# Layer 0's parameters moved, one more unsplit gate, and attention with two products per head and quarter turns

## The reference

```python
xn = rmsnorm(x, norm1_g)
cq, ckv, k_rope, u, gate_a, gate_b = split(xn @ w_in)        # 256, 128, 32, 512, 1024, 1024 columns
# branch A: 8 heads; q from cq, k (64 columns) and v (64) from ckv, 32 rotary columns shared in k
q, k = rmsnorm per head, rotary part turned
attn = softmax(q @ k.T / sqrt(96)) @ v ;  A = attn @ w_attn_up
# branch B: diagonal complex state space, 32 groups of 16 channels, 64 states, both directions
y = Re(C_f s_f) + Re(C_b s_b) + D * u ;  z = gelu(y) @ w_glu ;  B = z[:, :1024] * sigmoid(z[:, 1024:])
x = x + (sigmoid(gate_a) * A + sigmoid(gate_b) * B) @ w_o
x = x + (silu(h @ w_ffn_gate) * (h @ w_ffn_up)) @ w_ffn_down      # h = rmsnorm(x, norm2_g)
```

## Time and profile before

| | |
|---|---|
| median of 3 runs (range) | 1619.85 us (1618.29 to 1621.41) |
| the profiled execution | 1616.31 us, its span 1614.5 us |
| mean granted TensorE clock | 0.986 |
| busy: TensorE, VectorE, ScalarE, GpSimd | 1550.9, 884.8, 591.3, 557.8 us |
| instructions | 21071 |
| moved by DMA | 188.34 MB, mean 117 GB/s |

### The profile page before, as it was taken

The page is one execution under the profiler, slowest core; times in us unless marked ns, Lnnn a source line. Parts: engine busy times, 40 slices in busy tenths (PEclk is TensorE's granted clock), DMA queues, the critical chain, the costliest instruction groups (busy, mean ns, idle before and its releaser), DMA issues.

```text
span 1614.5 us, 21071 instructions
## 1 busy us (share of the span) xinstructions
PE 1550.9 (96%) x8352; PEld 1230.3 (76%) x8352; DVE 884.8 (55%) x1233; ACT 591.3 (37%) x992; POOL 557.8 (35%) x274
## 2 busy tenths in 40 slices
PE   8996998999999989999999899888999999999999
PEld 3554787778878877888888788777887888888887
DVE  5998477758547997558231862576684222112210
ACT  4561227653344231333331323676424223122220
POOL 0000013235434454434442333422434444434442
PEclk9998899999999999999999999999999999999999
DMA  7457720032232244453526362101422332322232
GB/s 253 157 173 258 277 88 1 1 105 91 92 120 91 79 148 155 147 160 91 169 96 246 117 231 89 50 1 40 118 79 91 105 104 82 101 91 95 88 104 79
DMA packets 73201, 188.34 MB, mean 117 GB/s; under 512 B 23568, under 2 KB 32144, under 8 KB 69008
## 3 DMA queue, kind: packets, MB, share of 16 engines
q1 hardware_dynamic: 43968, 145.18, 26.6%
q10 hardware_dynamic: 29136, 41.82, 8.0%
HBM read 154.47 MB, written 32.51 MB: 116 GB/s over the span
## 4 chain that ended last, share of the span: by engine, by line
PE 71%; DVE 15%; DVEq 5%; ACT 3%; DMA 2%; issue 2%; SPq 1%; POOL 0%; ACTq 0%; POOLq 0%
PE ps L1623 22%; PE ps L1624 22%; PE ps L1625 22%; PE ps L1767 2%; DVE qkTl L1479 1%; DVE nmx L1511 1%; DVE work L1036 1%; SPq L414 1%; ACT prob L945 1%; PE ps L1930 1%; DMA ctd_scr<-CPp 1%; PE ps L1921 1%; DVEq L1205 1%; DVEq L1163 1%; DVE work L1037 1%
## 5 line engine op out<-in xcount | busy, mean ns | idle before, releaser
L500 POOL TENSOR_TENSOR wl<-stage,wh 128x1024 fp32r<-128x1024 f32 x204 | 511.2, 2510 | 917.8 <-ACT wh L562 910.6
L562 ACT ACTIVATE wh<-stage 128x1024 fp32r<-128x1024 f32 x211 | 221.6, 1056 | 350.3 <-PE ps L1625 240.8
L1623 PE MATMUL ps<-xg2h,wh 128*128 128x512 f32 x704 | 280.7, 399 | 2.6 <-DVE act L1595 2.6
L1625 PE MATMUL ps<-xg2h,wl 128*128 128x512 f32 x704 | 279.1, 396 | 0.0
L1624 PE MATMUL ps<-xg2l,wh 128*128 128x512 f32 x704 | 279.0, 396 | 0.0
L1623 PEld LDWEIGHTS ps<-xg2h,wh 128*128 128x128 f32 x704 | 132.6, 188 | 35.5 <-issue 3.9
L1625 PEld LDWEIGHTS ps<-xg2h,wl 128*128 128x128 f32 x704 | 132.7, 188 | 32.2
L1624 PEld LDWEIGHTS ps<-xg2l,wh 128*128 128x128 f32 x704 | 132.8, 189 | 32.0 <-issue 0.5
L1623 PE MATMUL ps<-hidh,wh 128*128 128x512 f32 x352 | 139.8, 397 | 2.3 <-DVE hidl L1601 1.2
L1625 PE MATMUL ps<-hidh,wl 128*128 128x512 f32 x352 | 139.2, 396 | 0.0
L1624 PE MATMUL ps<-hidl,wh 128*128 128x512 f32 x352 | 139.2, 396 | 0.0
(11 more groups left out here) (271 smaller groups left out, 2840.4 us busy)
## 6 DMA issues: line engine op xcount, KB each, us to landing
stage<-in_stream SPq DMA_DIRECT2D x211, 512.0 KB, 3.2
CPTR<-ctd_scr ACTq DMA_DIRECT2D x6, 1664.0 KB, 10.3
slabs<-in_stream SPq DMA_DIRECT2D x16, 512.0 KB, 6.0
InT<-in_scr ACTq DMA_DIRECT2D x6, 1024.0 KB, 6.3
ctd_scr<-CPp SPq DMA_DIRECT2D x4, 1152.0 KB, 8.2
ctd_scr<-CPp ACTq DMA_DIRECT2D x4, 1152.0 KB, 6.6
in_scr<-BPI SPq DMA_DIRECT2D x4, 1024.0 KB, 5.1
in_scr<-BPI ACTq DMA_DIRECT2D x4, 1024.0 KB, 3.9
```

The lines of the kernel that those rows point to most:

```text
L500: pool.tensor_tensor(wl[:, s, :], stage[:, (n - RAW) % STAGES, :], wh[:, s, :].bitcast(F32), ALU.subtract).then_inc(wl_ready, 1)
L562: return act.activation(o, i, ACT.Copy, **kw)
L1623: pe.matmul(o, wt[0], x[0], start=start, stop=False)
L1625: return pe.matmul(o, wt[1], x[0], start=False, stop=stop)
```

## The change

Two groups of edits.

*Layer 0's front.* `RAW` becomes S_GATE + 10: slab 17 is an unsplit gate too. `BB`, `Call` and `pwi` move into the place of `xgl`, so VectorE's `normed_x` waits for the last taps (`k_ps`). `CPp`, `rot`, `pwc` lie in `CPTR[1]`'s place, `Kf` in `Toep[1]`'s; `InT[1]` and `U[1]` are free from the start, and SyncE loads them right after block 2's maps are stored. The taps of blocks 2 and 3 are stored from ScalarE's queue. Two slabs are loaded ahead of the waits in SyncE's queue. Inputs, outputs and states are set one gate later in the orders of TensorE and VectorE.

*Attention.* `vh` and `vl` become one tensor `vv` with four slots of 64 columns: high of head 0, low of head 0, low of head 1, high of head 1. A head's two slots together are one stationary operand of 128 columns; `pTh` and `pTl` pass through it once each. A bank then holds the high part's product in one half of the partitions and the low part's in the other. ScalarE copies the low half across (`other`), VectorE adds it (`added`), GpSimd scales (`scaled`) and makes `oTl` (`output`), but for the last pair, where VectorE does both. GpSimd also norms the keys of pairs 1 to 3. The probability-value product stands in odd units from 5 on. The turns come a quarter per unit, at units 3 to 6 on TensorE and ScalarE, 4 to 7 on VectorE. At the end the up projection's products of the first two slabs with pairs 0 to 2 are taken before the last pair's are ready, three of them before the last probability-value product.

```diff
-RAW = S_GATE + 9
+RAW = S_GATE + 10
...
-            ra = Region(ffn_top if l else set_at[1])
-            if l == 0:
-                CPp.append(ra.take(f"CPp{l}", [P, CPN]))
+            ra = Region(ffn_top if l else KT * SEQ * 4)
             BB.append(ra.take(f"BB{l}", [P, 2, C32, 2 * GCH]))
             Call.append(ra.take(f"Call{l}", [P, BLOCKS, 2, C8 * GCH]))
-            Kf.append(ra.take(f"Kf{l}", [P, 2, KW]))
+            pwi.append(ra.take(f"pwi{l}", [P, 2, C32, CHUNK]))
+            if l == 0:
+                assert ra.at <= XGB
+                ra = Region(set_at[1] + 4 * (INT + CTD))
+                Kf.append(ra.take(f"Kf{l}", [P, 2, KW]))
+                ra = Region(set_at[1] + 4 * INT)
+                CPp.append(ra.take(f"CPp{l}", [P, CPN]))
...
@@ SyncE
             store_cp(2)
+            load_input(1)
             store_turns()
-            store_input_map(3)
-            store_taps(2)
             load_output(0)
             load_taps(0)
+            store_input_map(3)
             store_cp(3)
-            for i in range(2):
-                sp.wait_ge(in_stored[i], 32)
+            staged_slab(RAW + 2)
+            staged_slab(RAW + 3)
             sp.wait_ge(k_ps, BLOCKS)
             sp.wait_ge(cp_stored, 16 * BLOCKS)
-            load_input(1)
             load_output(1)
-            store_taps(3)
             sp.wait_ge(k_stored, 128 * BLOCKS)
             load_taps(1)
...
@@ GpSimd
+                def normed_keys(hp):
+                    inv = ast[:, hp, 1, :].rearrange("p (t h) -> p t h", h=2)
+                    pool.wait_ge(qkT_ps, 4 * (PAIRS * l + hp))
+                    pool.tensor_tensor(KW_[:, :, :, 0:NOPE], ...)
+                    pool.tensor_tensor(KW_[:, :, :, NOPE:QK], ...)
+                    pool.drain().then_inc(k_normed, 1)
+
+                def scaled(hp):
+                    n = PAIRS * l + hp
+                    pool.wait_ge(r_copied, n + 1)
+                    pool.wait_ge(o_added, 2 * n + 2)
+                    pool.tensor_tensor(of[:], of[:], Rn[:], ALU.mult)
+                    pool.drain().then_inc(o_scaled, 1)
+
+                def output(hp):
+                    pool.wait_ge(oh_ready, PAIRS * l + hp + 1)
+                    pool.tensor_tensor(oTl[:, hp, :], of[:], oTh[:, hp, :].bitcast(F32), ALU.subtract).then_inc(o_ready, 1)
...
                         if u == 2:
                             rotated()
+                            normed_keys(hp + 1)
...
+                    if hp and a < STEPS:
+                        if u == 6:
+                            scaled(hp - 1)
+                    if a >= 2 * UNITS and u == 0:
+                        output(hp - 2)
...
@@ ScalarE
-                    split(0, S_GATE + 9)
+                    gain_slab(17)
+                    split(0, S_GATE + 10)
                     gate_out(6)
-                    split(0, S_GATE + 10)
+                    store_taps(0, 2)
+                    split(0, S_GATE + 11)
                     taps(0, 3)
                     gate_out(7)
-                    split(0, S_GATE + 11)
+                    store_taps(0, 3)
...
+                def other(hp, h):
+                    n = PAIRS * l + hp
+                    act.wait_ge(pv_done, 4 * n + 2 * h + 2)
...
+                    copy(oth[h * VD:(h + 1) * VD, :], ps[(1 - h) * VD:(2 - h) * VD, 4 + h, :]).then_inc(o_other, 1)
...
-                        if u in (4, 6):
-                            turned(hp + 1, u - 4)
+                        if 3 <= u < 7:
                             turned(hp + 1, u - 3)
...
+                    if a >= UNITS and u == 1:
+                        other(hp - 1, 0)
                     if a >= UNITS and u == 2:
                         scales(hp - 1)
                     if a >= UNITS and u == 4:
-                        output(hp - 1)
+                        other(hp - 1, 1)
+                    if a >= 2 * UNITS and u == 0:
+                        output(hp - 2)
...
@@ VectorE, layer 0
-                    remainder(S_GATE + 9)
                     remainder(S_GATE + 10)
+                    dve.wait_ge(k_ps, BLOCKS)
                     for k in range(KT):
                         normed_x(0, k)
                     direct_taps(0, 3)
                     dve.wait_ge(in_stored[0], 32)
                     gate(8)
+                    remainder(S_GATE + 11)
+                    gate(9)
                     states(0)
-                    gate(9)
-                    remainder(S_GATE + 11)
+                    gate(10)
                     remainder(S_GATE + 12)
                     states(1)
...
@@ VectorE, attention
+                def added(hp, h):
+                    n = PAIRS * l + hp
+                    half = slice(h * VD, (h + 1) * VD)
+                    if hp:
+                        dve.wait_ge(o_ready, n)
+                    dve.wait_ge(o_other, 2 * n + h + 1)
+                    tt(of[half, :], ps[half, 4 + h, :], oth[half, :], ADD).then_inc(o_added, 1)
...
+                    if a >= UNITS and u == 2:
+                        added(hp - 1, 0)
+                    if a < STEPS and hp and u == 5:
+                        added(hp - 1, 1)
+                    if a < STEPS and hp + 1 < PAIRS and u >= 4:
+                        turned(hp + 1, u - 4)
...
@@ TensorE, layer 0
                     inputs(0)
+                    gate(9)
                     for k in range(KT):
                         pe.wait_ge(xl_ready, k + 1)
-                    gate(9)
+                    gate(10)
                     inputs(1)
-                    gate(10)
+                    gate(11)
                     outputs(0)
-                    gate(11)
+                    gate(12)
                     outputs(1)
-                    gate(12)
                     inputs(2)
...
@@ TensorE, attention
-                        if hp + 1 < PAIRS and u in (4, 6):
-                            if u == 4 and hp:
+                        if hp + 1 < PAIRS and 3 <= u < 7:
+                            if u == 3 and hp:
                                 pe.wait_ge(r_copied, n)
-                            turn(hp + 1, (u - 4) // 2)
+                            turn(hp + 1, u - 3)
...
-                    if a >= 4 and a % 2 == 0:
-                        m = (a - 4) // 2
+                    if a == STEPS + 2:
+                        ready(S_UP)
...
+                        for k in range(PAIRS - 1):
+                            up_product(0, 0, k)
+                    if a >= 5 and a % 2:
+                        m = (a - 5) // 2
...
                         for t in range(TT):
-                            last = products(ps[:, 4 + h, tok], (vh[pair % 2][:, t, :], vl[pair % 2][:, t, :]),
-                                            (pTh[:, m % 2, t, :], pTl[:, m % 2, t, :]), t == 0, t == TT - 1)
+                            v = vv[pair % 2][:, t, 2 * h:2 * h + 2, :].rearrange("p a d -> p (a d)")
+                            pe.matmul(ps[:, 4 + h, tok], v, pTh[:, m % 2, t, :], start=(t == 0), stop=False)
+                            last = pe.matmul(ps[:, 4 + h, tok], v, pTl[:, m % 2, t, :], start=False, stop=(t == TT - 1))
                         last.then_inc(pv_done, 1)
```

More of the change, by code:

```diff
@@ L63 @@
 UP_ORDER = [(c, k) for c in range(2) for k in range(PAIRS)]
-UP_FIRST = [(c, k) for c in range(2) for k in range(PAIRS - 1)] + [(c, PAIRS - 1) for c in range(2)]
 QKV = 2 * (QK + NOPE + VD)
@@ L231, in build @@
         Rn = spare.take("Rn", [P, SEQ])
+        oth = spare.take("oth", [P, SEQ])
         of = RS
@@ L452, in _ @@
             sp.dma_start(Call[0][:].rearrange("p b r c -> p (b r c)"), cmat[0]).then_inc(call_loaded, 16)
-            for n in range(3, RAW - 1):
+            for n in range(3, RAW - 2):
                 raw(n)
             store_cp(0)
-            raw(RAW - 1)
+            raw(RAW - 2)
             staged_slab(RAW)
             staged_slab(RAW + 1)
+            raw(RAW - 1)
             store_input_map(0)
@@ L1894, in _, with up_product @@
                 pe.wait_ge(qk_sq, 8 * (l + 1))
-                turn(0, 0)
-                turn(0, 1)
+                for i in range(4):
+                    turn(0, i)
                 pe.wait_ge(qk_sqa, 8 * (l + 1))
-                for a in range(STEPS + 3):
+                def up_product(j, c, k):
+                    if j == 0:
+                        pe.wait_ge(o_ready, PAIRS * l + k + 1)
+                    return products(ps[:, 2 * j + c, :], weight(l, S_UP + j, k * 2 * P + c * P, P),
+                                    (oTh[:, k, :], oTl[:, k, :]), k == 0, k == PAIRS - 1)
+                for a in range(STEPS + 4):
                     hp, u = a // UNITS, a % UNITS
```

114 lines of the change are left out of this document (61 added, 53 removed).

## The result

The changed kernel took **1594.4 us** in the median of 4 runs (1593.2 to 1599.5), the kernel before 1619.1; ratio 0.986 (0.983 to 0.988). On two other chips, beside later experiments, it had 1602.1 (6 runs, ratio 0.990) and 1598.7 us (5 runs, 0.988). The profiled execution took 1599.5 us (span 1597.7 against 1614.5).

What follows compares the result with a forecast made beforehand. TensorE, busy 96% of the span, bounds the kernel, losing time mainly in layer 0's front and attention. 1616.3 - 22 (front) - 27 (attention) = 1567.3, plus 3.5 to the median: 1571 us, range 1560 to 1590.

Steps and rivals of the forecast that it cites:

- cost nothing unless the loads slip too: Layer 0's front: taps stores of blocks 2 and 3 from ScalarE's queue, some 5 us each, delay nothing TensorE needs soon.
- the slow clock's 10 us: Layer 0, 134 to 199 us: with the waits gone the low granted clock goes too, gaining 10 us.
- Rival 2: DMA still holds layer 0: block 1's states or maps late, about 10 us return, 1581 us; chance 0.12.
- The three waits of the earlier trace: Layer 0: TensorE's waits for `xgl` (5.48 us), `U` and `InT` (5.98) and `S` (3.45) vanish, 14.9 us.
- the sum of 22 us: Layer 0's front: net gain 23.5 us less 1.5 for new small waits; bounds 12 and 24.
- Rival 3: TensorE back to back, full gain in both parts (bounds 24 and 2 x 16): 1560 us; chance 0.08.
- Two products instead of three: Attention: eight probability-value matmuls a step for 12, 0.50 us less in 16 steps, 8.0 us of TensorE work per layer.
- the 5.5 forecast for the waits: Attention: lost time per layer goes from 17.7 to about 12.2 us; with 8.0 of work, 13.5 us per layer.
- The other 12.7 shrink to about 7: Attention: of 17.7 us lost per layer about 5 are pipeline filling and stay; the remaining waits shrink to about 7.
- lies under nine W_up products, a cost of zero there: Attention's tail: its longer chain, some 3.3 us, is covered by 6.3 us of products; 3 us if cover failed.
- rival 4: Attention: VectorE and GpSimd block each other at a shared port, period 8 us longer, 64 in all, 1635 us; chance 0.02.
- the narrow form: VectorE and GpSimd: port sharing hurts only VectorE instructions with two SBUF inputs, so the forecast of 1571 us stands.

Runs made afterwards that it cites:

- latents: Changed kernel with, in layer 0, the last block's Toep products ahead of the latents' third turn and VectorE's first turned latents made earlier; 1593.5 us.
- fronts: Changed kernel with block 2's taps stored from SyncE's queue, and Toep products and first turned latents moved earlier in both layers; 1585.4 us (0.979).
- all: Changed kernel with both layers' front edits, the gated-product edits and attention's reordered turns with VectorE's maximum left first; 1568.8 us (0.970).
- the taps kernel: Changed kernel with block 2's taps stores issued from SyncE's queue, ahead of block 0's output maps, instead of from ScalarE's; 1591.0 us (0.983).
- the third pass: Changed kernel with the first probability-value matmul issued twice, so 12 matmuls a step again; 1603.9 us (0.990).
- the order changed: Changed kernel with turn banks swapped, VectorE's turned remainder behind the maximum but ahead of additions, first addition and one GpSimd `oTl` later; 1593.9 us (0.985).
- the gated product kernel: Changed kernel with two `yT` loads ahead of the last `oTh`, `gyh` made by ScalarE, fourth Gelu ahead of a slab's split; 1598.7 us.

## Why the prediction was wrong, by its steps

**The taps stores "cost nothing unless the loads slip too": failed.** I looked for who stands behind the issuing, in ScalarE's queue, and priced that at nothing. The cost is at the landing: one `Kf`, so copy, addition and eviction of a gate wait for it. 7.7 us with the slow clock behind it (248.7 to 241.0 with the stores from SyncE), a net figure of two profiled executions: the wait of 1.93 us for `InT` goes too, and the pause for `latTl` grows by 2.0.

**Gain of the slow clock's 10 us, "a clock of 1.00 from 134 to 200": not met in the changed kernel (0.89 from 134 to 153, behind the wait for the gate's bank), met once the stores were moved, and then the loss stood further on.** With the three waits gone, TensorE reached the third turn of the latents before VectorE had made room; VectorE's last states step is stretched beside GpSimd's remainders (the scans and the first product behind them take 4.46 and 2.65 us at 203.3 and 207.9, in the block before 2.34 and 0.69). That this stretch makes the pause is argued, not tried; what was tried is the order of `latTl` and of the taps products, with which the pause is 0.1 us (latents), 0.7 (fronts) and 1.25 (all). The pause is 1.5 to 3.7 us, and in some executions the clock falls behind it: 7.0 us between the taps kernel and fronts (241.0 to 234.0). With 1.0 us left over, that is all of the front's 15.7. Rival 2 named DMA as the holder, at 10 us, through block 1's states or maps; half of the loss did hang on a DMA's landing, but on that of a store out of a single buffer, and the other half on VectorE's order.

**The front's other steps: right.** The three waits of the earlier trace rows are gone, `InT` is asked for early, and the sum of 22 us is met (234.0 against 233) by the kernel without those two. Rival 3's 1560 us was mis-added: bounds of 24 and 2 x 16 off the median of 1619.9 give 1564.

**Two products instead of three, 8.0 us of TensorE work a layer: right in work, but half of it was covered.** 64 matmuls are gone in each layer (529 to 461 in the stretch, with other groups' edges), a step of eight takes 1.03 us; putting them back costs 3.9. So this term, 8.0 in the sum, was worth 3.9 in the kernel as it ran: with the third pass back, the waits for `qkTl` (0.76 and 0.83 us) are gone, so without it they took part of the place of the work. That kernel with the third pass is still 5.8 and 5.5 us shorter than before to the first gated product, as the 5.5 forecast for the waits.

**"The other 12.7 shrink to about 7": too small by some 3.5 us.** This is the same shortfall seen from the other side. Named waits for `Rn` and `QW` came as priced (1.15 and 1.67 against 0.8 and 1.8). Missing were the waits at the second use of a turn bank, behind VectorE's addition in unit 5 (0.76 and 0.83 us, one in each of the third and fourth pair's turns). Attention gained 9.7 and 9.4 instead of 13.5; with the order changed, 13.2. The step was a sum over engine loads where a queue's order decided.

**The tail's longer chain "lies under nine W_up products, a cost of zero there": failed, with the wrong chain in view.** `oTl` is indeed covered. But those nine products (the prediction's count) had also covered what follows `o_ready`: the loads of `yT`, Gelu, `gyh`, `gyl`. From the last `oTl` to the first gated product it is 20.1 us before and 16.9 after; the fourth `gyl` ends 2.3 us late. Price 7.5 us in both layers together by the traces, taken out by the gated product kernel.

**The rule weighed.** `pTl` still takes 0.68 to 0.69 us, so rival 4 did not come. But the narrow form did matter at `gyl` and the scan, which read two operands from SBUF: `gyl` takes 2.75 us beside a remainder of GpSimd, 0.69 without. `gyh`, a cast with one input, from SBUF to SBUF, is stretched as well (2.58 against 0.41 to 0.43), which the narrow form as I had it doesn't cover. The kernel before has these long ones too (`gyl` 2.73 twice, `gyh` 2.54), under cover. The Trainium skill (SBUF — State Buffer, "Who interferes with whom") says that only VectorE's second port pair is shared with GpSimd and is locked exclusively; these rows agree. I applied it to the instructions that the change moved, not to those whose cover it took away.

**Sum.** Of 49 us forecast, taps 7.7, latents and clock 7.0, attention 7.9, the gated product 7.5: 30.1, which leaves 19; measured 16.8 between the profiled spans, 14 to 25 in the medians and 17 to 20 at full clock by the table. The terms are differences between single profiled executions; the changed kernel's own three profiles differ by up to 0.9 us in attention (99.9 to 100.8 in layer 0). Open is what decides whether the clock falls in a given execution, and why stores from ScalarE's queue landed 10 us later.

## What to carry to other kernels

When products are moved out of a tail to cover a chain, list everything that they covered before, up to the next stage's first operand: cover can't be spent twice. When stores move to another queue, look at who waits for their landing (the source buffer's next writer), not only at who stands behind their issue. In a loop of queues that are some 80% busy, leave the instruction that the next round waits for (here the maximum) first, and put what frees a bank ahead of what only accumulates.

## What the hardware showed that I had not expected

The same pause was followed by a low clock in one execution and not in the next: 1.47 us with it, 1.68 and 2.26 us without. Fourteen of the eighteen profiles have layer 0's latents in the first order, with this pause. Behind all seven pauses of 2.48 to 3.74 us the clock fell; behind the seven of 1.25 to 2.26 us it fell twice (1.26 and 1.47). With the fall it is 33.2 us to the first scores in all nine, without it 27.2 in all five. So a fall was rarer behind the shorter pauses, and not excluded. The changed kernel's profiled execution was 5 us above its median, and its two medians on two chips differed by 7.7 us (1594.4 and 1602.1) at mean clocks of 0.989 and 0.985; time x clock differs by 0.5 (1576.8 and 1577.3). It pays to compare this product beside the times. The Trainium skill (TensorE: Matmul & The Clock Gate, "The HAM clock gate (the "warmup" mystery)") says of the rise at a kernel's start that its point varies between runs of one kernel. No run here bears on the start; these rows show such a variation for the fall in mid-kernel.
